# Rotation left to the scores' contraction, the last down part in token halves, and two buffers placed at multiples of 2048 bytes

## The chip, the cores and the metric

The kernel runs on one core of one Trainium2 chip. The metric is the time of the device in microseconds for one launch; the time before is the median of three runs. TensorE is called PE below, VectorE DVE, ScalarE ACT, GpSimd POOL and SyncE SP, as the profile calls them.

## The reference, cut to what matters

One layer of a trunk, on a sequence of 512 tokens with 1024 channels, all in float32:

```python
x = x + 0.5 * swiglu(rms_norm(x, ffn1_norm), ffn1_w1, ffn1_w3, ffn1_w2)     # hidden width 2816
h = rms_norm(x, mix_norm)
proj = h @ w_in
c_q, c_kv, k_pe, q_s, k_s, v_s = jnp.split(proj, IN_SPLIT_POINTS, axis=-1)
y_mla = mla_attention(c_q, c_kv, k_pe, cos, sin, ...) @ w_o_mla             # 8 heads, 64 nope + 32 rope
y_swa = swa_attention(q_s, k_s, v_s, rel_bias, sinks) @ w_o_swa             # 16 heads, banded
g_mla, g_swa = jnp.split(sigmoid(h @ w_gate), 2, axis=-1)
x = x + (g_mla * y_mla + g_swa * y_swa) @ w_out
x = x + 0.5 * swiglu(rms_norm(x, ffn2_norm), ffn2_w1, ffn2_w3, ffn2_w2)
out = rms_norm(x, final_norm)
```

In the latent attention (MLA) a head's query is 64 plain numbers and 32 that are rotated: `q_pe = x1*cos - x2*sin, x2*cos + x1*sin`. The score of a query and a key is the sum over the 96. The rotated key is shared by all heads.

## The kernel before

The state x lies transposed, channels on the 128 partitions (8 tiles of 128x512, tokens along the free dimension). Each float32 product is made of three matmuls in the type float32r with a high and a low part of both operands (`three`, L1098: high by high L1101, weights' high by low L1102, weights' low by high L1103), each 128x128 weights by 128x512 moving, added in a PSUM bank. A "product" is one output tile: 8 such triples in the up projections, 8 or 6 in the down ones. A weight tile ("unit") is loaded by SP into one of four buffers `staged` (a load waits for `lo_done` of the unit four before), its high part is made by ACT (L508), its low part by DVE (L740), 1024 columns each, in two buffers `w_hi`, `w_lo`.

The program is in order: feed-forward 1 (PARTS of 8, 8 and 6 hidden tiles: for each part the up products, then 8 down products that are added to x), the mixing part, feed-forward 2 likewise, and the last norm. The hidden tiles are made by DVE (L802), rounded by ACT to `h_hi` (L531), and POOL makes `h_lo` (L395); `h_ready` counts POOL's.

In the mixing part the order is written out by hand: 48 steps of attention (16 banded, then 32 of MLA) run on PE, and behind each step PE does "fillers" of a plan (`fillers`, L63), products that have nothing to do with the step: latent projections, `kpe` (the shared rotary key), `uk`, `uv`, `uq` (the queries of head t, three triples), gates. In step n PE does the scores of step n + 2 (L1220 for MLA), the transposes of the probabilities of step n (L1252), the values, and the fillers. DVE in the same step normalises the probabilities of step n + 1 (L923, L924 for MLA), adds the mask and takes the maximum of step n + 2 (L901 to L903), splits a weight unit, and does its share of the fillers. For `uq` of head t, PSUM holds 64 plain rows, 32 rows of the rotary part and the same 32 swapped by halves. ACT copies the 64 rows (L668), DVE multiplies the 32 by the cosines (L984) and the swapped 32 by the signed sines into `rot` (L990), and POOL adds `rot` (L462, `q_ready`):

```python
nc.vector.tensor_tensor(qm[lo, t, :], b[lo, :], rope_sb[lo, :], ALU.mult)
...
dve.wait_ge(q_nope, t + 1)
nc.vector.tensor_tensor(rot[lo, :], b[hi, :], rope_sb[hi, :], ALU.mult).then_inc(grp_read, 1)
```

DVE's L990 of head t waits for ACT's copy of head t and for POOL's add of head t - 1. The scores read 96 rows of `qm` and `km`.

At the end, each of the 8 down products of the last part is added to x by DVE (L815); ACT squares it (L513) and scales it by the gain (L546); POOL adds the squares (L377). After the last one: PE sums over channels (L1154, L1393, one column each), DVE makes the variance (L754, L1088), POOL the power -0.5 (L387), DVE a Newton step (L770 to L773) and a diagonal (L775), PE spreads it over the partitions (L1162), ACT copies it (L732), DVE and POOL multiply the 8 tiles (L1094, L488), and SP sends them in six transfers (L360).

`h_hi` and `h_lo` start at an odd multiple of 64 bytes (a small tile `lead` is put in front and their alignment is 64), `lat_hi` and `lat_lo` at a multiple of 256; the other operands of the matmuls (`xg_hi`, `summed`, `om`, `w_hi`) start at multiples of LINE = 2048 bytes.

## Time and profile before

| | |
|---|---|
| median of 3 runs | 1160.23 us (1160.18 to 1160.59) |
| the profiled execution: its time | 1159.75 us |
| its span, first to last instruction | 1158.0 us |
| PE busy | 1127.8 us (97%) |
| DVE, ACT, POOL busy | 585.6, 400.9, 182.0 us |
| granted clock of PE, mean | 0.994 |
| chain that ended last | PE 91%, DVE 4%, ACT 2%, issue 1% |

The time of the profiled execution is 1.75 us more than its span, and 0.48 us under the median. A busy PE is not PE at its peak: records of matmuls overlap (each of 128x512 is shown as 0.39 us long while they start 0.23 us apart), so the pace of PE is read from starts. Weight loads (PEld) have records of their own.

### The profile page before, as it was taken

The numbers are of one execution on the slowest core, as the hardware profiler recorded it, in microseconds if no ns is written. First come the engines' busy times: TensorE is split into PE (matmuls) and PEld (weight loads), VectorE is DVE, ScalarE is ACT, GpSimd is POOL, SyncE is SP. The second block draws the span as 40 slices with busy tenths as digits, with TensorE's granted clock in tenths as the row PEclk, the third lists the DMA queues.
The fourth block names the chain that finished last, engine by engine and source line by source line (L and its number), as shares of the span: only waits on it lengthen the run. The fifth ranks groups of instructions, "written<-read, shape, count | busy, mean of one in ns | idle before, by whom it ended". The sixth has DMA issues, their size and how long they took to land.

```text
span 1158.0 us, 14717 instructions
## 1 busy us (share of the span) xinstructions
PE 1127.8 (97%) x5110; PEld 908.9 (78%) x5110; DVE 585.6 (51%) x870; ACT 400.9 (35%) x693; POOL 182.0 (16%) x134
## 2 busy tenths in 40 slices
PE   6999999999999999998999999999999999999995
PEld 4888888888888887765777788888888888888883
DVE  6644344433446436788555564545453344434444
ACT  5322123322325225584444433332231232222242
POOL 4111011100113103323000002231110011101133
PEclk9999999999999999999999999999999999999997
DMA  6234332333224321111222132222332322332221
GB/s 217 91 105 101 112 101 99 91 97 103 91 69 131 99 102 46 56 41 51 73 73 74 55 103 98 91 98 88 105 91 91 106 93 91 98 102 91 78 67 73
DMA packets 32301, 105.43 MB, mean 91 GB/s; under 512 B 3888, under 2 KB 5328, under 8 KB 32256
## 3 DMA queue, kind: packets, MB, share of 16 engines
q1 hardware_dynamic: 31824, 104.02, 27.9%
q0 software_dynamic: 192, 0.78, 0.6%
q8 instruction: 25, 0.41, 0.2%
q14 instruction: 20, 0.16, 0.0%
q10 hardware_dynamic: 240, 0.05, 0.0%
HBM read 101.96 MB, written 2.88 MB: 91 GB/s over the span
## 4 chain that ended last, share of the span: by engine, by line
PE 91%; DVE 4%; ACT 2%; issue 1%; POOL 0%; DMA 0%; DVEq 0%; SPq 0%; POOLq 0%; ACTq 0%
PE bank L1101 29%; PE bank L1103 28%; PE bank L1102 28%; PE bank L1220 1%; PE bank L1252 1%; PE bank L1277 1%; DVE xg_lo L747 1%; PE bank L1210 1%; ACT probs L607 1%; PE bank L1162 0%; DMA x<-in_x_t 0%; DVE w_lo L740 0%; DVE x L1094 0%; PE bank L1262 0%; DVE rot L990 0%
## 5 line engine op out<-in xcount | busy, mean ns | idle before, releaser
L1101 PE MATMUL bank<-xg_hi,w_hi 128*128 128x512 f32 (+1 forms) x1024 | 406.6, 397 | 10.1 <-DVE xg_lo L747 8.6
L508 ACT ACTIVATE w_hi<-staged 128x1024 fp32r<-128x1024 f32 x192 | 203.5, 1060 | 583.5 <-PE bank L1103 583.5
L1103 PE MATMUL bank<-xg_hi,w_lo 128*128 128x512 f32 (+1 forms) x1024 | 399.7, 390 | 0.0
L1102 PE MATMUL bank<-xg_lo,w_hi 128*128 128x512 f32 (+1 forms) x1024 | 399.7, 390 | 0.0
L740 DVE TENSOR_TENSOR w_lo<-staged,w_hi 128x1024 fp32r<-128x1024 f32 x192 | 236.7, 1233 | 101.2 <-ACT w_hi L508 100.9
L1101 PEld LDWEIGHTS bank<-xg_hi,w_hi 128*128 128x128 f32 (+1 forms) x1024 | 192.1, 188 | 58.9 <-issue 14.0
L1103 PEld LDWEIGHTS bank<-xg_hi,w_lo 128*128 128x128 f32 (+1 forms) x1024 | 192.3, 188 | 41.4
L1102 PEld LDWEIGHTS bank<-xg_lo,w_hi 128*128 128x128 f32 (+1 forms) x1024 | 192.4, 188 | 39.4 <-issue 0.7
L395 POOL TENSOR_TENSOR h_lo<-hid,h_hi 128x512 f32 x44 | 71.2, 1619 | 568.0 <-ACT h_hi L531 539.2
L1101 PE MATMUL bank<-h_hi,w_hi 128*128 128x512 f32 x352 | 138.8, 394 | 0.2
L1103 PE MATMUL bank<-h_hi,w_lo 128*128 128x512 f32 x352 | 137.7, 391 | 0.0
L1102 PE MATMUL bank<-h_lo,w_hi 128*128 128x512 f32 x352 | 137.2, 390 | 0.0
L815 DVE SCALAR_TENSOR_TENSOR x<-bank,x 128x512 f32 (+1 forms) x56 | 38.7, 691 | 152.9 <-PE bank L1103 152.9
L787 DVE TENSOR_TENSOR a_rms<-bank,rms 128x512 f32<-128x512 f32 x44 | 30.4, 691 | 118.9 <-PE bank L1103 118.8
L1103 PEld LDWEIGHTS bank<-h_hi,w_lo 128*128 128x128 f32 x352 | 66.1, 188 | 15.3
L1101 PEld LDWEIGHTS bank<-h_hi,w_hi 128*128 128x128 f32 x352 | 66.2, 188 | 14.7 <-POOL h_lo L395 1.1
L1102 PEld LDWEIGHTS bank<-h_lo,w_hi 128*128 128x128 f32 x352 | 66.1, 188 | 14.3
L377 POOL TENSOR_TENSOR acc<-acc,sq 128x512 f32<-128x512 f32 x36 | 56.9, 1580 | 95.3 <-ACT sq L513 84.4
L802 DVE TENSOR_TENSOR hid<-bank,silu 128x512 f32<-128x512 f32 x44 | 30.4, 692 | 79.1 <-PE bank L1103 78.7
L478 POOL TENSOR_TENSOR summed<-probs,summed 128x512 f32 x8 | 10.3, 1292 | 182.5 <-ACT summed L726 182.5
L620 ACT ACTIVATE probs_t<-bank 128x512 f32<-128x512 f32 (+3 forms) x48 | 23.4, 488 | 33.5 <-PE bank L1252 25.5
L792 DVE SCALAR_TENSOR_TENSOR silu<-silu,a_rms 128x512 f32<-128x512 f32 x44 | 31.6, 718 | 2.8 <-ACT silu L560 2.8
(131 smaller groups left out, 892.7 us busy)
## 6 DMA issues: line engine op xcount, KB each, us to landing
staged<-in_ffn_w SPq DMA_DIRECT2D x119, 512.0 KB, 3.3
staged<-in_w_gate SPq DMA_DIRECT2D x16, 512.0 KB, 3.3
staged<-in_w_in SPq DMA_DIRECT2D x15, 512.0 KB, 3.3
staged<-in_ffn_w SPq DMA_DIRECT2D x16, 384.0 KB, 3.1
staged<-in_w_ob SPq DMA_DIRECT2D x8, 512.0 KB, 3.3
staged<-in_w_out SPq DMA_DIRECT2D x8, 512.0 KB, 3.2
x<-in_x_t SPq DMA_DIRECT2D x8, 256.0 KB, 5.9
staged<-in_w_oa SPq DMA_DIRECT2D x4, 512.0 KB, 3.2
```

The costliest lines, as they stand in the source:

```text
L377: pool.tensor_tensor(acc[:, n % 2, :], acc[:, n % 2, :], sq[:, s % 2, :], ALU.add)\
L395: pool.tensor_tensor(h_lo[:, 2 * i + j, :], hid[:, (fb + j) % 2, :], h_hi[:, 2 * i + j, :].bitcast(f32), ALU.subtract)\
L508: nc.scalar.activation(w_hi[:, u % SPLIT, :], staged[:, u % STAGED, :], ACT.Copy).then_inc(hi_done, 1)
L620: nc.scalar.activation(probs_t[:, n % 2, 0:cols], bank[T_BANK + n % 2][:, 0:cols], ACT.Copy)\
L740: nc.vector.tensor_tensor(w_lo[:, u % SPLIT, :], staged[:, u % STAGED, :], w_hi[:, u % SPLIT, :].bitcast(f32), ALU.subtract).then_inc(lo_d ...
L787: nc.vector.tensor_tensor(a_rms[:, j, :], bank[g % 4][:, :], rms[:, :], ALU.mult).then_inc(grp_read, 1)
L792: nc.vector.scalar_tensor_tensor(out=silu[:, j, :], in0=silu[:, j, :], scalar=1.0, in1=a_rms[:, j, :], op0=ALU.add, op1=ALU.mult).then_inc ...
L802: nc.vector.tensor_tensor(hid[:, j, :], bank[g % 4][:, :], silu[:, j, :], ALU.mult).then_inc(grp_read, 1)
L815: nc.vector.scalar_tensor_tensor(out=x[:, k, :], in0=bank[(g + j) % 4][:, :], scalar=factor, in1=x[:, k, :], op0=ALU.mult, op1=ALU.add).th ...
L1101: nc.tensor.matmul(o, wh, hi, start=start, stop=False)
L1102: nc.tensor.matmul(o, wh, lo, start=False, stop=False)
L1103: return nc.tensor.matmul(o, wl, hi, start=False, stop=stop)
```

## The change

There are three edits.

**Rotation.** The weights of `uq` are as before, but `rope_sb` now holds ones in rows 0 to 63, cosines in 64 to 95 and signed sines in 96 to 127, and one multiplication of all 128 rows makes `qm`. The two rotary parts are not added; `km` holds the rotated key twice (rows 64 to 95 and 96 to 127), and the scores contract over 128 rows, which adds them. ACT's copy, DVE's second multiplication and POOL's addition are gone, with `q_nope` and `q_ready`. For the key, the `kpe` weights are 128 columns wide instead of 64, and DVE copies 64 rows for each head after a first copy of 32.

**Last down part.** Feed-forward 2's last down part is done for tokens 0 to 255 and then for 256 to 511 (`half`), each of its 16 products 18 matmuls of 256 columns. The split weights of all 8 units are kept in `end_hi` and `end_lo` (768 columns). The last norm of the first half is done between products of the second.

**Buffers.** `h_hi`, `h_lo`, `lat_hi` and `lat_lo` are aligned to LINE.

```diff
-            sb("lead", [P, 16], f32, ffn)
-            h_hi = sb("h_hi", [P, max(PARTS), S], f32r, ffn, align=64)
-            h_lo = sb("h_lo", [P, max(PARTS), S], f32r, ffn, align=64)
+            h_hi = sb("h_hi", [P, max(PARTS), S], f32r, ffn, align=LINE)
+            h_lo = sb("h_lo", [P, max(PARTS), S], f32r, ffn, align=LINE)
...
-            sb("lat_lead", [P, 64], f32, r)
-            lat_hi = sb("lat_hi", [P, 5, S], f32r, r, align=256)
-            lat_lo = sb("lat_lo", [P, 5, S], f32r, r, align=256)
+            lat_hi = sb("lat_hi", [P, 5, S], f32r, r, align=LINE)
+            lat_lo = sb("lat_lo", [P, 5, S], f32r, r, align=LINE)
...
-                elif kind == "uq":
-                    alone(q_ready, t + 1)
-                    pool.wait_ge(grp_read, MIX_G + G_UQ + t + 1)
-                    pool.tensor_tensor(qm[rope_rows, t, :], qm[rope_rows, t, :], rot[rope_rows, :], ALU.add)\
-                        .then_inc(q_ready, 1)
...
-                elif kind == "uq":
-                    act.wait_ge(grp_ready, g + G_UQ + t + 1)
-                    nc.scalar.activation(qm[0:NOPE, t, :], filler_bank(G_UQ + t)[0:NOPE, :], ACT.Copy)\
-                        .then_inc(q_nope, 1)
...
-                    nc.vector.tensor_tensor(qm[lo, t, :], b[lo, :], rope_sb[lo, :], ALU.mult)
-                    if t >= 1:
-                        dve.wait_ge(q_ready, t)
-                    else:
-                        dve.wait_ge(kpe_ready, 1)
-                    dve.wait_ge(q_nope, t + 1)
-                    nc.vector.tensor_tensor(rot[lo, :], b[hi, :], rope_sb[hi, :], ALU.mult).then_inc(grp_read, 1)
+                    nc.vector.tensor_tensor(qm[:, t, :], filler_bank(G_UQ + t)[:, :], rope_sb[:, :], ALU.mult)\
+                        .then_inc(grp_read, 1)
...
-                        pe.wait_ge(q_ready, h + 1)
-                        pe.wait_ge(kpe_ready, MH)
-                    rows = slice(0, NOPE + ROPE)
-                    nc.tensor.matmul(b[:, 0:query_keys(i)], qm[rows, h, norm_rows(i)], km[rows, h, 0:query_keys(i)],
+                        pe.wait_ge(grp_read, g + G_UQ + h + 1)
+                        pe.wait_ge(kpe_ready, MH + 1)
+                    nc.tensor.matmul(b[:, 0:query_keys(i)], qm[:, h, norm_rows(i)], km[:, h, 0:query_keys(i)],
                                      start=True, stop=True).then_inc(s_ready, 1)
...
+            def end_product(half, k):
+                n = KD * half + k
+                pe.wait_ge(lo_done, LAST_U + k + 1)
+                if n < 4:
+                    pe.wait_ge(grp_read, LAST_G - 3 + n)
+                else:
+                    pe.wait_ge(end_read, n - 3)
+                o = bank[(LAST_G + n) % 4][:, 0:HALF]
+                for f in range(LAST_F):
+                    if n == 0:
+                        pe.wait_ge(h_ready, 2 * sum(PARTS) - LAST_F + f + 1)
+                    w_cols = slice(f * P, (f + 1) * P)
+                    hi, lo = h_hi[:, f, half_cols(half)], h_lo[:, f, half_cols(half)]
+                    nc.tensor.matmul(o, end_hi[:, k, w_cols], hi, start=f == 0, stop=False)
+                    nc.tensor.matmul(o, end_hi[:, k, w_cols], lo, start=False, stop=False)
+                    last = nc.tensor.matmul(o, end_lo[:, k, w_cols], hi, start=False, stop=f == LAST_F - 1)
+                last.then_inc(end_ready, 1)
...
+            for half in range(HALVES):
+                for k in range(KD):
+                    end_product(half, k)
+                    if half == 1 and k == 1:
+                        sum_end(0)
+                    if half == 1 and k == 3:
+                        spread_end(0)
+            sum_end(1)
+            spread_end(1)
```

ACT in the end, for each half and tile, and DVE and POOL likewise:

```python
            for half in range(HALVES):
                for k in range(KD):
                    if half == 0 and k + AHEAD < KD:
                        end_split(k + AHEAD)
                    n = KD * half + k
                    act.wait_ge(end_read, n + 1)
                    if k >= 2:
                        act.wait_ge(end_acc, (KD - 1) * half + k - 1)
...
                    nc.scalar.activation(sq_end[:, k % 2, :], x[:, k, half_cols(half)], ACT.Square).then_inc(end_sq, 1)
                    nc.scalar.activation(x[:, k, half_cols(half)], x[:, k, half_cols(half)], ACT.Copy,
                                         scale=gain[:, 3 * KD + k, :]).then_inc(out_scaled, 1)
                    if half == 1 and k == 4:
                        read_rms_end(0)
            read_rms_end(1)
```

**Where instructions move.** DVE in one step of MLA with a `uq` filler, before (L923, L924 normalise, L901 to L903 mask and maximum, L984 and L990 the filler):

```order
L923 RECIPROCAL rden<-den 128x1
L924 TENSOR_SCALAR probs<-probs,rden 128x256
L901 TENSOR_TENSOR bank<-bank,mask_sb 128x128
L902 TENSOR_REDUCE smax<-bank 128x1
L903 TENSOR_SCALAR nmax<-smax 128x1
L740 TENSOR_TENSOR w_lo<-staged,w_hi 128x1024
L984 TENSOR_TENSOR qm<-bank,rope_sb 32x512
L990 TENSOR_TENSOR rot<-bank,rope_sb 32x512
```

The same step after:

```order
L989 RECIPROCAL rden<-den 128x1
L990 TENSOR_SCALAR probs<-probs,rden 128x256
L967 TENSOR_TENSOR bank<-bank,mask_sb 128x128
L968 TENSOR_REDUCE smax<-bank 128x1
L969 TENSOR_SCALAR nmax<-smax 128x1
L806 TENSOR_TENSOR w_lo<-staged,w_hi 128x1024
L1052 TENSOR_TENSOR qm<-bank,rope_sb 128x512
```

One of the filler's two instructions is gone, and the other has 128 rows instead of 32; POOL's `L462 TENSOR_TENSOR qm<-qm,rot 32x512` (8 of them) and ACT's 8 copies are gone too.

PE at the end of the program, before, from the last triple on:

```order
L1101 MATMUL bank<-h_hi,w_hi 128x512
L1102 MATMUL bank<-h_lo,w_hi 128x512
L1103 MATMUL bank<-h_hi,w_lo 128x512
L258 REGISTER_ALU
L258 COMPARE_AND_BRANCH
L1154 MATMUL bank<-one,acc 128x1 x4
L1393 MATMUL bank<-one,sq 128x1 x4
L1162 MATMUL bank<-diag,one 128x512
```

And after:

```order
L1510 MATMUL bank<-h_hi,end_hi 128x256
L1511 MATMUL bank<-h_lo,end_hi 128x256
L1512 MATMUL bank<-h_hi,end_lo 128x256
L1518 MATMUL bank<-one,acc_end 128x1 x2
L1523 MATMUL bank<-one,sq_end 128x1 x2
L1530 MATMUL bank<-diag,one 128x256
```

The last three rows stand in this place for the second half alone; the same for the first half stands between products of the second: L1518 and L1523 behind its second product, L1530 behind its fourth.

DVE at the end, before, from the last read of a product on:

```order
L815 SCALAR_TENSOR_TENSOR x<-bank,x 128x512 x2
L754 TENSOR_SCALAR var<-bank 128x4
L1088 SCALAR_TENSOR_TENSOR var<-bank,var 128x4
L770 TENSOR_TENSOR corr<-rstd 128x4
L771 SCALAR_TENSOR_TENSOR corr<-corr,var 128x4
L773 SCALAR_TENSOR_TENSOR rstd<-corr,rstd 128x4
L775 TENSOR_TENSOR diag<-idn,rstd 128x512
L1094 TENSOR_TENSOR x<-x,rms 128x512 x6
```

And after, from the third product of the second half on:

```order
L1193 SCALAR_TENSOR_TENSOR x<-bank,x 128x256 x4
L1184 TENSOR_TENSOR x<-x,rms 128x256 x6
L1193 SCALAR_TENSOR_TENSOR x<-bank,x 128x256 x2
L1164 TENSOR_SCALAR var<-bank 128x2
L1168 SCALAR_TENSOR_TENSOR var<-bank,var 128x2
L1171 TENSOR_TENSOR corr<-rstd 128x2
L1172 SCALAR_TENSOR_TENSOR corr<-corr,var 128x2
L1174 SCALAR_TENSOR_TENSOR rstd<-corr,rstd 128x2
L1176 TENSOR_TENSOR diag<-idn,rstd 128x256
L1184 TENSOR_TENSOR x<-x,rms 128x256 x6
```

The six multiplications of the first half (L1184) now stand ahead of the reads of the last two products.

## Rows read from the trace of the kernel before

**Rows 1.** Timeline of PE, an up part: start us, us, engine, line, operation.
```profile
925.43 0.39 PE L1101 MATMUL bank<-xg_hi,w_hi 128*128 128x512 f32 x1
...
939.71 0.39 PE L1101 MATMUL bank<-xg_hi,w_hi 128*128 128x512 f32 x1
```
**Rows 2.** Timeline of PE, a down part.
```profile
1005.08 0.39 PE L1101 MATMUL bank<-h_hi,w_hi 128*128 128x512 f32 x1
...
1019.50 0.39 PE L1101 MATMUL bank<-h_hi,w_hi 128*128 128x512 f32 x1
```
**Rows 3.** Busy time in a stretch: width, PE, PEld, DVE, ACT, POOL, PE's clock.
```profile
505.00:548.00 43.00, 36.94 (x177) 25.87 (x176) 36.01 (x75) 24.23 (x72) 14.27 (x12) 1.00 0.13 44
```
**Rows 4.** Groups of 505 to 548 us: busy us, mean ns, idle before.
```profile
L462 POOL TENSOR_TENSOR qm<-qm,rot 32x512 f32<-32x512 f32 x8 | 10.1, 1264 | 23.2 <-DVE rot L990 23.2
...
L990 DVE TENSOR_TENSOR rot<-bank,rope_sb 32x512 f32<-32x512 f32 x8 | 5.6, 696 | 2.3 <-ACT qm L668 1.7 <-POOL qm L462 0.5
L984 DVE TENSOR_TENSOR qm<-bank,rope_sb 32x512 f32<-32x512 f32 x8 | 5.5, 689 | 2.7 <-ACT vm L665 2.2 <-PE bank L1103 0.2
...
L902 DVE TENSOR_REDUCE smax<-bank 128x1 f32<-128x256 f32 x2 | 0.8, 424 | 0.1
```
**Rows 5.** Timeline of one `uq` step, and of a later L924 with POOL idle.
```profile
535.00 0.81 PE L1220 MATMUL bank<-km,qm 96*128 96x384 f32 x2
...
535.57 1.25 POOL L462 TENSOR_TENSOR qm<-qm,rot 32x512 f32<-32x512 f32 x1 [3.08 <-DVE rot L990]
535.66 1.32 DVE L924 TENSOR_SCALAR probs<-probs,rden 128x256 f32<-128x256 f32 x1
...
537.03 0.44 PE L1252 MATMUL bank<-idn,probs 128*128 128x128 f32 x2 [1.23 <-DVE probs L924]
...
549.12 0.42 DVE L924 TENSOR_SCALAR probs<-probs,rden 128x384 f32<-128x384 f32 x1
```
**Rows 6.** Timeline: the start of the last down part.
```profile
1106.80 0.40 PE L1101 MATMUL bank<-h_hi,w_hi 128*128 128x512 f32 x1
...
1108.83 1.65 POOL L395 TENSOR_TENSOR h_lo<-hid,h_hi 128x512 f32 x1 [9.24 <-ACT h_hi L531]
...
1110.53 0.50 PE L1101 MATMUL bank<-h_hi,w_hi 128*128 128x512 f32 x1
```
**Rows 7.** Page, groups: ACT's split of a unit.
```profile
L508 ACT ACTIVATE w_hi<-staged 128x1024 fp32r<-128x1024 f32 x192 | 203.5, 1060 | 583.5 <-PE bank L1103 583.5
```
**Rows 8.** Chain of work: sums and spread behind the first feed-forward (start, us, what).
```profile
388.14 0.79 PE bank L1154 x8
...
394.54 0.86 PE bank L1162 x2
```
**Rows 9.** Timeline: the end of the program.
```profile
1139.95 0.39 PE L1103 MATMUL bank<-h_hi,w_lo 128*128 128x512 f32 x1
...
1140.37 0.69 DVE L815 SCALAR_TENSOR_TENSOR x<-bank,x 128x512 f32<-128x512 f32 x1 [3.43 <-PE bank L1103]
1141.16 0.63 ACT L513 ACTIVATE sq<-x 128x512 f32<-128x512 f32 x1 [2.87 <-DVE x L815]
...
1141.84 0.97 PEld L1393 LDWEIGHTS bank<-one,sq 128*128 128x128 f32 x8 [0.80 <-ACT sq L513]
...
1143.24 1.02 POOL L387 TENSOR_TENSOR rstd<-var,minus_half 128x4 f32<-128x4 f32 x1 [4.14 <-DVE var L1088]
...
1144.88 0.69 DVE L775 TENSOR_TENSOR diag<-idn,rstd 128x512 f32<-128x512 f32 x1
...
1145.63 2.08 PE L1162 MATMUL bank<-diag,one 128*128 128x512 f32 x2 [2.74 <-DVE diag L775]
1147.74 0.60 ACT L732 ACTIVATE rms<-bank 128x512 f32<-128x512 f32 x1 [5.34 <-PE bank L1162]
1148.37 5.84 DVE L1094 TENSOR_TENSOR x<-x,rms 128x512 f32<-128x512 f32 x6 [2.80 <-ACT rms L732]
```
**Rows 10.** Busy time in a stretch, as in rows 3: the spread of the last norm.
```profile
1145.60:1148.00 2.40, 2.08 (x2) 0.50 (x2) 0.00 (x0) 0.26 (x1) 0.00 (x0) 0.50 0.01 3
```

More of the change, by code:

```diff
@@ L247, in trunk_layer @@
         POOL_OUT = (6, 7)
+        DVE_OUT = tuple(k for k in range(KD) if k not in POOL_OUT)
+        END_SUM, END_RMS = (7, 5), (6, 4)
+        END_COLS = TT // HALVES
         M_SCALE = float(NOPE + ROPE) ** -0.5
@@ L401, in ffn_program @@
                         bring()
-                clear_acc(n)
-                if n == NORM_OUT:
-                    for t in range(KD - 1):
-                        add_square(n, t)
-                else:
+                if n is not None:
+                    clear_acc(n)
                     loop(pool, 2, lambda i: [add_square(n, t, i) for t in range(4)], first=1)
@@ L1290, in next_bank, with half_product @@
                 return filler_bank(r)
-            def half_product(uu, r, half, width=P):
+            def half_product(uu, r, half):
                 if half == 0:
@@ L1297, in half_product @@
                 for k in range(4 * half, 4 * half + 4):
-                    last = three(filler_bank(r)[0:width, :], slice(k * width, (k + 1) * width), uu, *from_x(k),
-                                 k == 0, k == KD - 1)
+                    last = three(filler_bank(r)[:, :], slice(k * P, (k + 1) * P), uu, *from_x(k), k == 0, k == KD - 1)
                 if half == 1:
@@ L1389, in _ @@
             ffn_program(FFN2_U, FFN2_G, sum(PARTS), 2, NORM_X2)
-            sum_squares(NORM_OUT)
-            pe.wait_ge(sq_done, sq_base[NORM_OUT + 1])
-            for t in range(TT):
-                last = nc.tensor.matmul(bank[RMS_BANK][:, t:t + 1], sq[:, (sq_base[NORM_OUT + 1] - 1) % 2, norm_rows(t)],
-                                        one[:, 0:1], start=True, stop=True)
-            last.then_inc(ss_ready, 1)
-            spread_rms(NORM_OUT)
+            def end_product(half, k):
+                n = KD * half + k
+                pe.wait_ge(lo_done, LAST_U + k + 1)
[13 more added lines that the diff above has]
+                last.then_inc(end_ready, 1)
@@ new lines, in sum_end @@
+            def sum_end(half):
+                pe.wait_ge(end_acc, (KD - 1) * (half + 1))
+                for t in range(END_COLS):
+                    last = nc.tensor.matmul(bank[END_SUM[half]][:, t:t + 1], acc_end[:, half, norm_rows(t)], one[:, 0:1],
+                                            start=True, stop=True)
+                last.then_inc(end_summed, 1)
+                pe.wait_ge(end_sq, KD * (half + 1))
+                for t in range(END_COLS):
+                    last = nc.tensor.matmul(bank[END_RMS[half]][:, t:t + 1], sq_end[:, (KD - 1) % 2, norm_rows(t)],
+                                            one[:, 0:1], start=True, stop=True)
+                last.then_inc(end_summed, 1)
@@ new lines, in spread_end @@
+            def spread_end(half):
+                pe.wait_ge(end_diag, half + 1)
+                cols = diag[:, half * END_COLS:(half + 1) * END_COLS, :].rearrange("p a b -> p (a b)")
+                nc.tensor.matmul(bank[END_RMS[half]][:, 0:HALF], one[:, :], cols, start=True, stop=True)\
+                    .then_inc(end_spread, 1)
+            for half in range(HALVES):
+                for k in range(KD):
+                    end_product(half, k)
+                    if half == 1 and k == 1:
+                        sum_end(0)
+                    if half == 1 and k == 3:
+                        spread_end(0)
```

220 lines of the change are left out of this document (157 added, 63 removed).

## The prediction

> **What bounds the kernel now.** I read the page first. PE is busy for 97% of the span and makes 91% of the chain that ended last, and its clock is full nearly throughout. So the kernel is a stream of matmuls, and only three things can move its time: the pace of the stream, the places where it stops, and what lies behind its last matmul.
>
> The pace is read from starts in the timeline of PE. In an up part, the first and the last row of [rows 1] are 63 matmuls apart (21 triples): 14.28 us, 226.7 ns each. In a down part [rows 2] the same 63 take 14.42 us, 228.9 ns each. The weights come from the same buffers in both; the moving operand is `xg`, at a multiple of 2048 bytes, in the first and `h`, at a multiple of 64, in the second. Neither stretch has a wait in it.
>
> The stops come from the busy time by stretch. From 505 to 548 us, where the `uq` fillers are, PE is busy for 36.94 of 43 us, and DVE for 36.01 [rows 3]. The timeline of one step [rows 5] shows why: PE has done its scores (two passes from 535.00, 0.65 us by the 0.81 shown less the overlapping drain), and the transposes start at 537.03, since DVE's L924 ends only at 536.98. That L924 took 1.32 us for 256 columns; with POOL idle the same instruction took 0.42 for 384. It overlaps POOL's L462 (535.57 to 536.82), so the two hold each other up. DVE is therefore late by its own two filler instructions (0.69 and 0.70 us) and by about 1.0 us that POOL costs it [rows 4, 5].
>
> The end is in [rows 9]: the last matmul of the down part starts at 1139.95 and is over at 1140.34. The span ends at 1158.0, so 17.7 us lie behind it, a chain through all engines on tiles of 512 tokens.
>
> **The change, term by term.** The sum is made against the profiled execution (1159.75 us; span 1158.0), which lies 0.48 us under the median of the runs.
>
> *Buffers.* The two feed-forwards have 1056 matmuls that read `h`; 912 of them keep 512 columns. If the 2.2 ns come from where `h` starts, they save 912 x 2.2 = 2.0 us. Bounds: 0 (the cause is another) and 2.3 (`lat` gains likewise). I take **-2.0**, because both stretches are without waits and differ in the moving operand alone.
>
> *Rotation.* Of a `uq` step DVE loses L990 (0.70) and its wait for ACT's copy, and L924 loses POOL's company (about 1.0). The instruction that stays is as long with 128 rows as with 32, by the nearest rows: L984 on 32 rows takes 689 ns [rows 4] and L775 on 128 rows 0.69 us [rows 9]. Over 8 heads this is some 13 us of DVE's 36, so DVE has 23 us of work in a stretch in which PE has 37. PE can get back at most its idle 6.1 us (43 - 36.94) [rows 3]; none at least, if another wait takes its place. A step's latency (maximum, exponential, normalisation) is spread over two steps, so I take nearly all: **-5.5**. The wider `kpe` weights and one more copy of the key fall where PE was not idle; I cost them at nothing, and at 0.7 us (one DVE instruction [rows 4]) if DVE's slack there is used up.
>
> *Late hidden tile.* The first product of the last down part needs the sixth hidden tile behind 15 matmuls. Before, that is at 1106.80 + 15 x 0.229 = 1110.24, and POOL's `h_lo` ends at 1110.48, so PE went on at 1110.53 after a stop of 0.29 [rows 6]. Now 15 matmuls of half the length are over at 1108.5, and the tile is still made for all 512 tokens. The stop becomes 2.0: **+1.7** (1.4 if ACT, which no longer waits for a free `w_hi`, rounds the tile earlier; 2.3 if POOL is held up by DVE's four splits in a row).
>
> *Pace at 256 columns.* 288 matmuls take the place of 144 at 228.9 ns (33.0 us). The stream alone would allow half of 226.7, 113.3 ns. Each also needs its own 128x128 weights. The loads behind one another at the end [rows 9] are 8 in 0.97 us, the last 0.19 long: (0.97 - 0.19)/7 = 111 ns apart. So the floor is 111. The other bound: at 512 columns each start is 13.4 ns more than 512 columns at 2.4 GHz (213.3); if that is a price of each matmul rather than of each column, 256 columns take 120. Between 111 and 120 I take 116: 33.4 us, **+0.4** (-1.0 to +1.6).
>
> Here a rule speaks against the change. The rows show loads hidden under the stream: at 226.7 ns apart there is no room for 213 of columns and 111 of weights [rows 1, 9]. The Trainium skill (TensorE: Matmul & The Clock Gate, Part 3, "The mechanism") says that loads overlap running matmuls only where the row groups differ, and all here use all rows; by that each matmul would pay for both. The trace at 512 columns disagrees with it; at 256 columns no row shows it, and it stands as a rival below.
>
> *Inserted work.* Between products of the second half PE now does the sums of the first (8 one-column passes, like L1154 x8: 0.79) and its spread at half width (half of L1162's 0.86 at full clock) [rows 8]: 1.2, and 0.1 for each change of kind, **+1.4** (1.2 to 2.0). DVE's and ACT's work on the first half lies beside PE's products. What is queued behind DVE's first norm (its waits for PE's sums and POOL's power, about 2.5 us) is the read of the third product, which PE needs free only two products later.
>
> *The end.* From the end of the last matmul, the new chain: read of 256 columns 0.45 (a DVE instruction on 256 columns takes 0.42 [rows 4]); 0.35 late, since DVE has just done six multiplications of the first half and ACT's squares lag; square 0.5; sums 0.7; to POOL's start 0.4; power 1.0; Newton step 0.6; diagonal 0.45; spread 1.2, half of 2.08 and a little, if PE's clock has dropped to 1.2 GHz by then as it had before [rows 10]; copy 0.4; multiplications half of 5.84, 2.9; from there to the end of the span 3.8 before (1158.0 - 1154.2), and with transfers of 384 KB in place of 512 I take 3.6 [rows 9]. The sum is 12.55, for 17.7: 5.1 less. I take **-5.0** (-3.5 if the first half's work makes the last reads 1.5 us late; -6.0 if the spread is at full clock and the transfers gain more).
>
> *Weights of the last part.* A product now takes 18 x 0.116 = 2.1 us instead of 4.1, and in the first half ACT must split a unit (768 columns: 0.85 by L508's 1.06 for 1024 [rows 7]), square and scale: 1.75. DVE needs 0.95 and 0.42. Both fit under 2.1; four units are split ahead. Nothing is charged.
>
> Sum: -2.0 - 5.5 + 1.7 + 0.4 + 1.4 - 5.0 = **-9.0 us**, 1150.75 for a profiled execution, and 1160.23 - 9.0 = **1151.2** for the median.
>
> **The rivals.**
>
> *A (the mixing part keeps its stops).* PE's wait for the probabilities could turn into one for the exponentials, ACT being in the same loop. For it: ACT's splits of 1.06 us stand in the same steps. Against: ACT was busy for only 24.2 of the 43 us. Then the rotation gives 1.5 instead of 5.5: 1155.2.
>
> *B (no gain from the buffers).* 2.2 ns could come from how a down part is built (6 or 8 triples a product). Against: the extra is in every triple, not at a product's start. Then 1153.2.
>
> *C (the last part is bound by its weights or by ACT).* At 1.75 of 2.1 us ACT has 0.35 to spare, and loads of 384 KB now have to come every 2.1 us. If four products are late by 1 us each: 1155.2.
>
> *D (slower: loads stop being hidden).* A load's record is 188 ns long, and if the next matmul waits for its end, the spacing is about 188: 288 x (188 - 116) = +20.7, 1172. If stream and load come one after another (113 + 111 = 224), it is 288 x 108 = +31, 1182; this is what the rule above would give. Against the first: loads start 111 ns apart while 0.19 long. D decides from a spacing of 116 + 9000/288 = 147 ns on; under that the change stays faster.
>
> *E (nothing comes of it).* Rotation and end both give half: 2.7 + 2.5 + 2.0 - 3.5 = 3.7 less, 1156.5; with dearer inserted work it comes within 0.2% (2.3 us, about what a measurement of this kernel can tell from no change).
>
> **How the numbers follow.** Forecast 0.56, A 0.12, B 0.10, C 0.06, D 0.07 (stream and load one after another 0.02 of it), E 0.09. The bounds of the terms give the forecast 1148 to 1154 (buffers 0.3, rotation 0.6, late tile 0.6, pace 1.3, end 1.5, taken together and not all on one side). Holding A, B, C and most of E and the low bounds a little further, the range is 1146.5 to 1157.0. Faster is all but D and a half of E: 0.88; same (the other half) 0.05; slower 0.07.
>
> **What would show it.** Right: matmuls of a down part 226.7 ns apart; PE busy for all of the `uq` stretch and L990 (the old L924) at 0.4 us; POOL without the additions; a stop of about 2 us before the sixth triple of the last part; 256-column matmuls 111 to 120 ns apart; 12 to 13 us behind the last of them. Wrong: `h` still at 228.9; transposes waiting for DVE or ACT in the `uq` steps; a spacing of 147 ns or more; ACT or a load as what ends PE's waits in the last part.

## The result and the profile after

| | before | after |
|---|---|---|
| median of the runs | 1160.41 us (1160.18 to 1160.61, 4 runs) | 1148.55 us (1147.53 to 1149.57, 4 runs) |
| profiled execution: time, span | 1159.75, 1158.0 us | 1149.52, 1147.7 us |
| PE busy | 1127.8 us (97%) | 1125.6 us (98%) |
| POOL, DVE busy | 182.0, 585.6 us | 170.5, 574.7 us |

The ratio is 0.9899, with an interval of 0.9887 to 0.9911: the changed kernel is 1.0% faster, 11.9 us by the medians. 1151.2 was forecast, in a range of 1146.5 to 1157.0. One of the 15 runs of the kernel before beside experiments 7 and 8 took 1267.34 us, at a granted clock of 0.848, and is left out of their ratios.

The stretch of [rows 3], the same 43 us of the profile after (columns as there):

```profile
505.00:548.00 43.00, 42.98 (x219) 32.03 (x219) 30.47 (x80) 24.43 (x73) 4.05 (x4) 1.00 0.15 52
```

PE has no stop left in it, and POOL's additions are gone. The normalisation of the probabilities on DVE (L924 before, L990 now), by form, in the same stretch:

```profile
L990 DVE TENSOR_SCALAR probs<-probs,rden 128x384 f32<-128x384 f32 x2 | 0.8, 420 | 0.1
```

It takes 0.42 us for 384 columns; 256 of them took 1.32 beside POOL's addition [rows 5].

A down part, timeline of PE, against [rows 2]: 63 matmuls in 14.28 us, 226.7 ns each.

```profile
1002.00 0.39 PE L1208 MATMUL bank<-h_hi,w_hi 128*128 128x512 f32 x1
...
1016.28 0.39 PE L1208 MATMUL bank<-h_hi,w_hi 128*128 128x512 f32 x1
```

The last down part, timeline: its first matmul, POOL's making of the sixth hidden tile, the matmul that waited for it, 36 matmuls of the stream (120.0 ns each), and the work inserted between products of the second half.

```profile
1097.88 0.28 PE L1510 MATMUL bank<-h_hi,end_hi 128*128 128x256 f32 x1
...
1099.63 1.27 POOL L415 TENSOR_TENSOR h_lo<-hid,h_hi 128x512 f32 x1 [8.91 <-ACT h_hi L568]
...
1100.96 0.39 PE L1510 MATMUL bank<-h_hi,end_hi 128*128 128x256 f32 x1 [1.13 <-POOL h_lo L415]
...
1115.10 0.28 PE L1510 MATMUL bank<-h_hi,end_hi 128*128 128x256 f32 x1
...
1119.42 0.28 PE L1510 MATMUL bank<-h_hi,end_hi 128*128 128x256 f32 x1
...
1120.86 0.50 PE L1518 MATMUL bank<-one,acc_end 128*128 128x1 f32 x4
1121.22 0.58 PE L1523 MATMUL bank<-one,sq_end 128*128 128x1 f32 x4
1121.67 0.36 PE L1510 MATMUL bank<-h_hi,end_hi 128*128 128x256 f32 x1
...
1126.06 0.60 PE L1530 MATMUL bank<-diag,one 128*128 128x256 f32 x2
```

The end, timeline, against [rows 9]:

```profile
1135.01 0.28 PE L1512 MATMUL bank<-h_hi,end_lo 128*128 128x256 f32 x1
...
1135.32 0.42 DVE L1193 SCALAR_TENSOR_TENSOR x<-bank,x 128x256 f32<-128x256 f32 x1 [0.52 <-PE bank L1512]
...
1135.78 0.42 ACT L787 ACTIVATE sq_end<-x 128x256 f32<-128x256 f32 x1
...
1137.51 0.71 POOL L509 TENSOR_TENSOR rstd<-var,minus_half 128x2 f32<-128x2 f32 x1 [1.45 <-DVE var L1168]
...
1139.32 1.22 PE L1530 MATMUL bank<-diag,one 128*128 128x256 f32 x2 [2.15 <-DVE diag L1176]
...
1140.99 3.16 DVE L1184 TENSOR_TENSOR x<-x,rms 128x256 f32<-128x256 f32 x6 [1.73 <-ACT rms L772]
```

From the end of the last matmul (1135.28) to that of the span 12.4 us are left, where there were 17.7.

### The profile page after: what moved, and what is told of

Same layout as the page of the kernel before. It is cut to its first block, busy times and chain, and to the rows that moved or that the text cites. A ratio compares the mean times of both kernels' runs of the same rounds, so it can differ in the third digit from the quotient of the medians.

```text
span 1147.7 us, 14995 instructions
## 1 busy us (share of the span) xinstructions
PE 1125.6 (98%) x5256; PEld 918.0 (80%) x5256; DVE 574.7 (50%) x883; ACT 398.6 (35%) x702; POOL 170.5 (15%) x136
## 4 chain that ended last, share of the span: by engine, by line
PE 95%; DVE 3%; ACT 1%; issue 0%; DMA 0%; POOL 0%; DVEq 0%; SPq 0%; POOLq 0%; ACTq 0%
PE bank L1208 29%; PE bank L1210 28%; PE bank L1209 28%; PE bank L1328 2%; PE bank L1360 1%; PE bank L1385 1%; PE bank L1319 1%; PE bank L1510 1%; DVE xg_lo L813 1%; PE bank L1512 1%; PE bank L1511 1%; PE bank L1370 1%; DVE x L1184 0%; DMA staged<-in_ffn_w 0%; PE bank L1269 0%
## 5 line engine op out<-in xcount | busy, mean ns | idle before, releaser
L1208 PE MATMUL bank<-xg_hi,w_hi 128*128 128x512 f32 x1024 | 406.8, 397 | 10.1 <-DVE xg_lo L813 8.6
L1210 PE MATMUL bank<-xg_hi,w_lo 128*128 128x512 f32 x1024 | 399.7, 390 | 0.0
L1209 PE MATMUL bank<-xg_lo,w_hi 128*128 128x512 f32 x1024 | 399.6, 390 | 0.0
L1208 PEld LDWEIGHTS bank<-xg_hi,w_hi 128*128 128x128 f32 x1024 | 192.6, 188 | 59.1 <-issue 14.2
L1210 PEld LDWEIGHTS bank<-xg_hi,w_lo 128*128 128x128 f32 x1024 | 192.6, 188 | 40.9
L1209 PEld LDWEIGHTS bank<-xg_lo,w_hi 128*128 128x128 f32 x1024 | 192.8, 188 | 39.1 <-issue 0.7
L415 POOL TENSOR_TENSOR h_lo<-hid,h_hi 128x512 f32 x44 | 70.8, 1610 | 565.4 <-ACT h_hi L568 537.0
L1208 PE MATMUL bank<-h_hi,w_hi 128*128 128x512 f32 x304 | 118.4, 389 | 0.2 <-POOL h_lo L415 0.2
L1209 PE MATMUL bank<-h_lo,w_hi 128*128 128x512 f32 x304 | 118.3, 389 | 0.0
L1210 PE MATMUL bank<-h_hi,w_lo 128*128 128x512 f32 x304 | 118.3, 389 | 0.0
L881 DVE SCALAR_TENSOR_TENSOR x<-bank,x 128x512 f32 x48 | 33.2, 691 | 134.7 <-PE bank L1210 134.7
L1208 PEld LDWEIGHTS bank<-h_hi,w_hi 128*128 128x128 f32 x304 | 57.1, 188 | 12.4 <-POOL h_lo L415 0.6
L1209 PEld LDWEIGHTS bank<-h_lo,w_hi 128*128 128x128 f32 x304 | 57.1, 188 | 11.9
```

What stands on the lines that cost most here:

```text
L415: pool.tensor_tensor(h_lo[:, 2 * i + j, :], hid[:, (fb + j) % 2, :], h_hi[:, 2 * i + j, :].bitcast(f32), ALU.subtract)\
L881: nc.vector.scalar_tensor_tensor(out=x[:, k, :], in0=bank[(g + j) % 4][:, :], scalar=factor, in1=x[:, k, :], op0=ALU.mult, op1=ALU.add).th ...
L1208: nc.tensor.matmul(o, wh, hi, start=start, stop=False)
L1209: nc.tensor.matmul(o, wh, lo, start=False, stop=False)
L1210: return nc.tensor.matmul(o, wl, hi, start=False, stop=stop)
```

## The experiments

Medians of kernels on different chips differ by more than some of the effects. So two lengths are read from each profiled execution as well: **A**, from the start of the fifth `xg_lo` on DVE (13.90 us in the profile before) to the end of the span, and **B**, the middle part, from the last addition to x of feed-forward 1 (377.36) to the first of the attention's output (741.90). Two executions of the changed kernel agree in both within 0.1 us.

| kernel | A, us | B, us |
|---|---|---|
| before | 1144.1 | 364.5 |
| buffers alone | 1142.6 | 365.7 (clock) |
| last part alone | 1143.4 | 365.7 (clock) |
| rotation alone | 1137.0 | 357.6 |
| rotation, POOL's addition back | 1138.1 | 358.7 |
| rotation, DVE's multiplication back | 1138.7 | 359.3 |
| rotation, both back | 1141.1 | 361.3 |
| rotation, both and ACT's copy back | 1144.2 | 364.8 (clock) |
| changed; again | 1133.5; 1133.5 | 357.6; 357.6 |
| changed, two products together | 1132.3 | 357.6 |

"(clock)": PE's granted clock fell to half for a while at 523 us. It costs 1.15 us of B (365.7 - 364.5, in two kernels that leave that part's order alone), and is told of below. A "stop" is an idle time of PE of 0.1 us or more in the stretch of [rows 3]; the one near 505 us, for DVE's `lat`, is in all kernels and is not counted.

**1. Buffers alone.**

```diff
-            h_hi = sb("h_hi", [P, max(PARTS), S], f32r, ffn, align=64)
+            h_hi = sb("h_hi", [P, max(PARTS), S], f32r, ffn, align=LINE)
...
-            lat_hi = sb("lat_hi", [P, 5, S], f32r, r, align=256)
+            lat_hi = sb("lat_hi", [P, 5, S], f32r, r, align=LINE)
```

> The kernel before with the third edit alone: h and lat at multiples of 2048 bytes. Theory (where the moving operand starts sets the pace): every matmul on h is 226.7 ns behind the last instead of 228.9, 1056 of them, so 2.3 us less, about 1158.0. Rival (the pace in a down part comes from how a down product is built, and the change got its gain elsewhere): 228.9 stays and the time is 1160.3.

Measured: 1157.68 us (10 runs) beside 1161.12 (19 runs), ratio 0.9975 (0.9965 to 0.9984). The same 63 matmuls of a down part, timeline of PE:

```profile
1003.18 0.39 PE L1099 MATMUL bank<-h_hi,w_hi 128*128 128x512 f32 x1
...
1017.46 0.39 PE L1099 MATMUL bank<-h_hi,w_hi 128*128 128x512 f32 x1
```

226.7 ns each: where `h` starts is the cause of the 2.2 ns. The products on `lat` did not change: nine matmuls from 514.2 us on are 228.8 ns apart before and nine from 513.1 us on 228.6 here. A is 1.5 less, and 2.6 with the clock's 1.15 taken out.

**2. Rotation alone.**

> The kernel before with the first edit alone. Theory (the stops of the uq steps are all DVE being late, by its second filler instruction and by POOL's addition): PE is busy for 43 of the 43 us from 505 to 548 and the time falls by 6.9 us, what the trace of the changed kernel shows between the end of the first feed-forward and the last values of the attention: about 1153.4. Rival (part of it was from the buffer lat or came with the other edits): 1154.5 to 1157.

Measured: 1153.43 us (4 runs) beside 1161.12, ratio 0.9942 (0.9926 to 0.9959); B is 6.9 us less. Busy time of the stretch with the same 177 records of PE as [rows 3]:

```profile
505.40:541.50 36.10, 35.58 (x177) 26.28 (x177) 26.74 (x71) 21.24 (x66) 4.17 (x4) 1.00 0.19 64
```

43.00 us have become 36.10, and that is all of B's gain. PE's idle time went from 6.06 to 0.52 us, and its busy time fell by 1.36 too, for the same matmuls.

The kernel before has seven stops in its stretch that are gone here. Three, in steps of MLA (537.03, 542.12 and 546.83, together 3.25 us), end with DVE's L924, as the prediction read from one step. The other four, 2.62 us together, end with POOL. They are in the last two banded steps, in which POOL makes the normalisation (L442), in its program order behind the addition of `uq` (L462). This is the second of them, in the kernel before:

```profile
521.16 1.26 POOL L462 TENSOR_TENSOR qm<-qm,rot 32x512 f32<-32x512 f32 x1 [3.34 <-DVE rot L990]
521.24 0.18 DVE L918 RECIPROCAL rden<-den 128x4 f32<-128x4 f32 x1
...
522.49 1.04 POOL L442 TENSOR_TENSOR probs<-probs,rden 128x512 f32<-128x512 f32 x1
522.52 0.46 PE L1220 MATMUL bank<-km,qm 96*128 96x128 f32 x2 [1.14 <-issue]
...
523.59 0.66 PE L1252 MATMUL bank<-idn,probs 128*128 128x128 f32 x4 [0.61 <-POOL probs L442]
```

L442 has its operand at 521.42 and starts at 522.49, behind L462. The stop of 1.14 us ends with L462 too: these are a head's first scores, in front of which the program waits for `q_ready`, and they start 0.1 us after L462's end. In the step before, the two stops are 0.26 and 0.61 us.

**3. Last part alone.**

> The kernel before with the second edit alone, h where it was. Theory: the last part costs 4.0 us more up to its last matmul (288 starts 120 ns apart in place of 144 at 228.9: +1.6; late hidden tile +1.0; sums and spread of the first half +1.3) and 5.3 us less lie behind it: -1.3, about 1159.0, perhaps less if the half steps are dearer with h at 64 bytes. Rival (the gain behind the last matmul is bigger in unprofiled runs, which for the changed kernel came out at 1147.5 or at 1149.5): two groups of times 2 us apart, 1157 and 1159.

Measured: 1159.24 us (10 runs) beside 1161.12, ratio 0.9989 (0.9979 to 0.9998). A is 0.7 less, 1.8 with the clock's 1.15 taken out. That is 0.4 more than the edit gives in the changed kernel (its terms below sum to -1.4). Here `h` still starts off by 64 bytes, and 36 matmuls of the last part (timeline of PE) are 117.8 ns apart in place of 120.0; experiment 9 takes this up. The ten runs lie in two groups, 1157.98 to 1158.40 (four, with a mean granted clock of 0.996) and 1159.00 to 1159.85 (six, with 0.995, the profiled one among them), so that the fall of the clock at 523 us (1.15 us) is nearly enough to tell them apart; the rival's groups, 2 us apart by what lies behind the last matmul, are not shown.

```profile
1115.23 0.28 PE L1527 MATMUL bank<-h_hi,end_hi 128*128 128x256 f32 x1
...
1119.47 0.28 PE L1527 MATMUL bank<-h_hi,end_hi 128*128 128x256 f32 x1
```

**4. The pace by itself.** Behind the spread of the last norm:

```diff
+            def run(count, cols, off, w=P, w_off=0):
+                for m in range(count):
...
+                    nc.tensor.matmul(bank[m // 12 % 4][0:w, 0:cols], wt[:, 0, w_off + tile * P:w_off + tile * P + w],
+                                     mv[:, tile * S + off:tile * S + off + cols], start=True, stop=True)
```

> The kernel before with 17 rows of matmuls added behind its last one, whose results nobody reads: 512, 384, 256, 192, 128 and 64 moving columns, moving operands that start 4, 16, 64, 256 columns off a multiple of 512 columns, weights of 64 columns, weights that start off a multiple of 128 columns. Theory (a matmul costs its columns at 2.4 GHz and a fixed 13.4 ns, and never less than the load of its weights, 111 ns): 226.7, 173.4, 120.0, then 111 for 192 (93.4), 128 and 64. Rival (the extra is 1/16 of the columns): 226.7, 170, 113.3, 111. With a start off the multiple by 16 or 64 columns: 228 to 230 by the theory of the buffers, 226.7 by its rival.

Measured, mean spacing of starts in a series (weights of 128 columns, start at a multiple of 2048 bytes, where nothing else is said):

| series | ns |
|---|---|
| 512, 384, 256 columns | 226.7, 173.3, 120.0 |
| 192, 128 columns | 111.7, 111.7 |
| 512 columns, moving operand off by 16, 64, 256, 1024 bytes | 231.6, 228.9, 226.7, 226.7 |
| 512 columns, weights off by 64, 256 bytes | 233.4, 226.7 |
| 512, 256 columns, weights of 64 columns | 230.0, 113.3 |

The series at 256 bytes starts with ten matmuls some 232 ns apart, behind the slower series before it, and is at 226.7 from then on.

From 512 to 256 columns the spacing falls by 106.7 ns, which is 256 columns at 2.4 GHz; so each matmul costs its columns and a fixed 13.3 ns, and the other way of sharing the 13.4 ns out (a price of each column), which the prediction gave weight, is refuted. At 192 and 128 columns the floor of 111.7 rules. What the fixed price is paid for is not shown: with weights of half as many columns it goes at 256 moving columns (113.3 ns), and at 512 it does not (230.0 ns, more than with full weights). Rival D is refuted: a matmul of 256 columns is 120.0 ns after the last with a load of 128x128 of its own, not 188 and not 113 + 111. With it falls, for these matmuls that use all rows, the rule of the Trainium skill (TensorE: Matmul & The Clock Gate, Part 3, "The mechanism") that was weighed in the prediction.

**5. POOL's addition back.** The rotation alone, and on POOL behind each `uq`:

```diff
+                elif kind == "uq":
+                    alone(spare_done, t + 1)
+                    pool.wait_ge(grp_read, MIX_G + G_UQ + t + 1)
+                    pool.tensor_tensor(rot[rope_rows, :], rot[rope_rows, :], rot[rope_rows, :], ALU.add)\
+                        .then_inc(spare_done, 1)
```

> The rotation alone (as in the run before), and POOL has an addition of 32x512 again behind every one of the 8 uq fillers, in a tile that nobody reads; it is work that is added, nothing is left out. Theory: POOL's addition and DVE's normalisation of the probabilities hold each other up, and this is the larger part of what the rotation gave. Then the normalisation in the uq steps goes from 0.37 back to about 1.3 us, the addition takes 1.25 instead of some 0.4 to 1.0, and the kernel is 1.5 to 4 us slower than the rotation alone. Rival: what counted was DVE's second multiplication and its waits, and PE's slack of about 1.2 us in these steps takes the 0.9 us in; then it is under 0.8 us slower, though the normalisation is at 1.3 us again.

Measured: 1154.32 us (4 runs) beside 1160.07 (7 runs), ratio 0.9951 (0.9934 to 0.9967); B is 1.1 us over the rotation alone. The stretch of [rows 3] and the group of the normalisation in it:

```profile
505.00:548.00 43.00, 41.73 (x201) 30.42 (x201) 33.98 (x79) 24.10 (x71) 12.42 (x12) 1.00 0.19 62
```
```profile
L920 DVE TENSOR_SCALAR probs<-probs,rden 128x128 f32<-128x128 f32 (+3 forms) x7 | 6.7, 960 | 0.2
```

0.96 us in the mean in place of 0.37: the hold-up is back, and PE does not feel it, for no step of MLA has a stop. The 1.1 us come from POOL's other work. There are two stops, 0.17 and 0.57 us, in the last two banded steps, where POOL's normalisation again stands behind its addition (the second of them):

```profile
519.80 1.03 POOL L462 TENSOR_TENSOR rot<-rot 32x512 f32<-32x512 f32 x1 [2.17 <-DVE qm L982]
...
520.91 1.04 POOL L442 TENSOR_TENSOR probs<-probs,rden 128x512 f32<-128x512 f32 x1
...
522.01 0.66 PE L1244 MATMUL bank<-idn,probs 128*128 128x128 f32 x4 [0.57 <-POOL probs L442]
```

The theory that the hold-up of DVE is the larger part of the gain falls.

**6. DVE's second multiplication back**, without POOL's addition:

```diff
+                    nc.vector.tensor_tensor(rot[NOPE:NOPE + ROPE, :], filler_bank(G_UQ + t)[NOPE + ROPE:P, :],
+                                            rope_sb[NOPE + ROPE:P, :], ALU.mult).then_inc(grp_read, 1)
```

> The rotation alone, and DVE has its second multiplication of 32x512 again behind every uq filler, in a tile that nobody reads, without ACT's copy and without POOL's addition; it is work that is added, nothing is left out. Theory (the lock of POOL and DVE is the larger part): 8 x 0.70 = 5.6 us more of DVE's work meet a slack of about 1.2 us in every step, and the kernel is 0 to 1.5 us slower than the rotation alone. Rival (DVE's work as such is the larger part): 1.5 to 4 us slower, with PE waiting for the normalised probabilities again. Third way: neither this nor POOL's addition alone costs over 0.8 us, and the stops came only from both together.

Measured: 1154.63 us (4 runs), ratio 0.9954 (0.9937 to 0.997); B 1.6 us over the rotation alone.

```profile
505.00:548.00 43.00, 41.84 (x202) 30.68 (x201) 35.35 (x84) 24.51 (x73) 4.12 (x4) 1.00 0.16 55
```

It is not the larger part either: 1.1 and 1.6, of 6.9. Again no step of MLA has a stop. The two stops, 0.11 and 1.03 us, are in the last two banded steps, where POOL's normalisation waits for DVE's L908, which comes later.

**7. Both back** (the edits of 5 and 6, and DVE's next one waits for POOL's last):

> The rotation alone, with both additions of the two runs before it: DVE's second multiplication and, behind it, POOL's addition, each in a tile that nobody reads; DVE's next one waits for POOL's last one as it did before the change. It is work that is added, nothing is left out. From the start of the attention steps on, POOL's addition alone cost 1.1 us and DVE's multiplication alone 1.6; the whole that the rotation took away is worth 6.9. Theory: the two costs lie behind one slack in every step (about 1.2 us), so each alone is mostly hidden and both together are not: 0.7 + 0.95 a step less the slack. Then the middle part is 4.5 to 7 us longer than in the rotation alone, and the normalisation is at 1.3 us in every uq step. Rival: the costs simply add to 2.7 us, and the other 4 us of the rotation come from something else: ACT's copy of 64 rows and DVE's wait for it.

Measured: 1156.99 us (6 runs) beside 1160.85 (15 runs), ratio 0.9967 (0.9955 to 0.998); B 3.7 us over the rotation alone, between the 2.7 of a plain sum and the 4.5 that the theory wanted at least. The stops are 0.87 and 1.30 us in the banded steps and 0.95 in one step of MLA, for DVE's normalisation; with either alone that step had none.

```profile
505.00:548.00 43.00, 39.49 (x189) 28.67 (x190) 37.48 (x81) 21.99 (x68) 12.42 (x12) 1.00 0.16 56
```

**8. Both and ACT's copy of 64 rows**, with DVE's wait for it:

```diff
+                elif kind == "uq":
+                    act.wait_ge(grp_ready, g + G_UQ + t + 1)
+                    nc.scalar.activation(qm[0:NOPE, t, :], filler_bank(G_UQ + t)[0:NOPE, :], ACT.Copy)\
+                        .then_inc(copied, 1)
...
+                    dve.wait_ge(copied, t + 1)
```

> As the run before it, and ACT copies the 64 plain rows again (DVE multiplies only the other 64), with DVE's second multiplication waiting for the copy. What is left of the rotation edit is the contraction over 128 rows and the wider key; nothing is left out. Theory: ACT's copy of 0.58 us ends 0.2 us after DVE's first multiplication started beside it and adds 0 to 1.5 us to the run with both; the middle part comes within 1 us of that of the kernel before (6.9 us over the rotation alone). Rival: ACT's copy is where the missing 4 us were, and this run is 3 us or more over the one with both.

Measured: 1158.99 us (10 runs) beside 1160.85, ratio 0.9987 (0.9978 to 0.9997). B is 364.8, 363.6 with the clock's 1.15 taken out: 6.0 over the rotation alone, 0.9 short of the kernel before. ACT's copy with its wait is worth 2.3 us on top of both, more than the theory allowed (1.5) and less than the rival wanted (3). So no part carries the gain alone: taken back one after another they cost 1.1 (POOL), 2.6 (DVE on top), 2.3 (ACT's copy on top) and 0.9 (the rest). That rest goes with POOL's additions: on one tile they take 1.03 us here, on two 1.26 before [rows 4], and the normalisation is held up less, 1.09 for 1.32; that this is all of it was not tried. The stops say where it lies. In the banded steps they are as long here (0.87 and 1.76 us) as before (0.87 and 1.75), though PE's own wait for POOL's addition, `q_ready`, is not back; so that wait costs nothing. In the three steps of MLA they are 0.28, 1.14 and 0.44 us, where the kernel with the buffers alone, which had the same fall of the clock, has 0.81, 1.36 and 0.66: 0.97 less.

**9. Starts and widths.** As 4, with other series:

> The kernel before, with 492 further matmuls of 128x128 weights whose results nobody reads, between the spread of the last norm and its use, in series of 36 with one width and one start of the moving operand: it is work that is added, nothing is left out. Open is why the last part runs at 117.8 ns a matmul of 256 columns where h starts at an odd multiple of 64 bytes (the run with the last part alone) and at 120.0 where it starts at a multiple of 2048. Theory: the start counts at 256 columns too, but the other way round: 118 ns for a start off by 64 bytes and 120 for one off by 0, with 226.7 and 228.9 at 512 columns again. Rival: the start has nothing to do with it and the 2 ns come from what runs beside the last part, or from the changing weights; then all series of 256 columns are at 120.0.

Measured: the theory's numbers. Timeline of PE, pairs of rows 24 matmuls apart, 256 columns with a start off by 0 and by 64 bytes, and 512 with a start off by 0, 64 and 128 bytes:

```profile
1164.31 0.28 PE L1405 MATMUL bank<-xg_hi,w_hi 128*128 128x256 f32 x1
...
1167.19 0.28 PE L1405 MATMUL bank<-xg_hi,w_hi 128*128 128x256 f32 x1
...
1168.62 0.28 PE L1405 MATMUL bank<-xg_hi,w_hi 128*128 128x256 f32 x1
...
1171.45 0.28 PE L1405 MATMUL bank<-xg_hi,w_hi 128*128 128x256 f32 x1
...
1203.17 0.39 PE L1405 MATMUL bank<-xg_hi,w_hi 128*128 128x512 f32 x1
...
1208.61 0.39 PE L1405 MATMUL bank<-xg_hi,w_hi 128*128 128x512 f32 x1
...
1211.36 0.39 PE L1405 MATMUL bank<-xg_hi,w_hi 128*128 128x512 f32 x1
...
1216.85 0.39 PE L1405 MATMUL bank<-xg_hi,w_hi 128*128 128x512 f32 x1
...
1219.62 0.39 PE L1405 MATMUL bank<-xg_hi,w_hi 128*128 128x512 f32 x1
...
1225.20 0.40 PE L1405 MATMUL bank<-xg_hi,w_hi 128*128 128x512 f32 x1
```

That is 120.0, 117.8, 226.7, 228.8 and 232.5 ns. At 384 columns both starts give 173.3. So the edit of the buffers costs the last part 288 x 2.2 = 0.6 us of what it gives elsewhere.

**10. The late hidden tile out of the way**, in the changed kernel:

```diff
+            end_product(0, 0, range(LAST_F - 1))
+            end_product(0, 1, range(LAST_F - 1))
+            end_product(0, 0, (LAST_F - 1,))
+            end_product(0, 1, (LAST_F - 1,))
```

> The changed kernel, with the sixth hidden tile's triples of the first two products of the last down part done together: five tiles of product 0, five of product 1, then the sixth of each. Nothing is left out. The stop before the sixth tile is 1.29 us in the changed kernel (15 matmuls are over at 1099.7, the tile is there at 1100.9). With 30 matmuls ahead of it, PE gets there at 1097.9 + 30 x 0.120 = 1101.5, 0.6 us after the tile, so the stop should go to nothing: 1.3 us less than the changed kernel run beside it. Rival: the first reads by DVE and squares by ACT come 0.4 us later, and that or a weight unit that is split late gives the time back further on; then the two kernels are the same within 0.5 us, with a new wait for DVE or ACT in the first half of the last part.

Measured: 1146.84 us (4 runs: three at 1146.8, one at 1148.23) beside 1149.17 for the changed kernel, ratio to before 0.989 (0.9873 to 0.9906). A is 1.2 us less, as the theory had it, and the idle time before the group of the last part's first matmuls, 1.1 us in the changed kernel, is gone:

```profile
L1510 PE MATMUL bank<-h_hi,end_hi 128*128 128x256 f32 x95 | 27.3, 287 | 0.0
```

The other 1.1 us of the 2.3 lie in the first 14 us of the program and are told next.

**11. The changed kernel again.**

> The changed kernel again, unaltered, beside the others. Its four runs lay in two groups, 1147.5 and 1149.5 us. Theory: the two groups are its own and not the chip's, so it shows them here too, 2 us apart, and the profile of one of the lower group would show the place. Rival: they were the chip's, and all runs here lie within 0.5 us of each other.

Measured: 1149.17 us (1149.14 to 1149.65, 4 runs), ratio 0.9907 (0.9891 to 0.9924). All four lie within 0.5 us and none at 1147.5: the theory that the two groups are the kernel's own is not borne out, and no trace shows the lower group. The timeline of the first weight splits still shows one way in which executions come apart. POOL and DVE here:

```profile
11.39 1.48 POOL L395 TENSOR_TENSOR acc<-acc,sq 128x512 f32<-128x512 f32 x1 [0.23 <-ACT sq L550]
11.64 2.31 DVE L806 TENSOR_TENSOR w_lo<-staged,w_hi 128x1024 fp32r<-128x1024 f32 x1
```

And in the profile of experiment 10:

```profile
11.59 1.21 DVE L806 TENSOR_TENSOR w_lo<-staged,w_hi 128x1024 fp32r<-128x1024 f32 x1
...
12.09 1.86 POOL L395 TENSOR_TENSOR acc<-acc,sq 128x512 f32<-128x512 f32 x1 [0.97 <-ACT sq L550]
```

Where POOL is first, DVE's split ends 1.08 us after POOL's operation (13.95 and 12.87); where DVE is first, POOL's ends 1.15 after the split. The start of the program, where tiles of x arrive by DMA, decides which is first, and everything behind is 1.1 us earlier or later.

## Why the prediction came out right, step by step

The profiled executions differ by 10.2 us (A by 10.6), where the sum said 9.0. The medians differ by 11.9: most of before's runs in these comparisons lie between 1160 and 1161.5 us and the profile of before at 1159.75, so the profile that the sum was made against was one of the quicker ones. That of the changed kernel, 1149.52, was one of its slower ones; the median of 1148.55 lies between the two groups. That the sum of the terms is off by 1.6 us and the median by 2.7 is in part this choice of executions.

- **Buffers, -2.0.** Right in mechanism and size: 1.2 us less up to the end of feed-forward 1, and 1.0 in feed-forward 2 up to the last part, -2.2. Rival B is refuted by experiment 1.
- **Rotation, -5.5: the term mis-sized most, -6.9.** The step that failed is the bound, "PE can get back at most its idle 6.1 us". It got back 5.5 of these and 1.4 that the rows show as busy. A record of 0.39 us outlasts the 0.227 after which the next one starts; at a stop these 0.16 us are no longer covered by a next record. Seven stops went, 7 x 0.16 = 1.1. The second matmul behind a stop was late by another 0.06 to 0.08 us when the starts of both kernels are compared one by one, together 0.4: 1.5, about the 1.4 measured. That the stops go and no other wait takes their place came true, and rival A is refuted by the stretch without a stop. The account of what made them was right in part. The step that was read, at 535 us, stands for three steps of MLA and 3.25 us; the other 2.62 us were for POOL's own instructions in two banded steps (experiment 2). The price of POOL's company was charged in all 8 steps, though L924 stands in the stretch only five times: DVE lost 9.3 us of busy time (36.01 to 26.74), not 13. Experiments 5 to 8 show three parts: POOL's addition, DVE's multiplication and ACT's copy. Neither of the first two gives a stop in a step of MLA when it is alone; together they give one, and with the copy three.
- **Late hidden tile, +1.7.** Measured 1.3 of stop in place of 0.3, +1.0: POOL's L415 began 1.75 us behind the part's first matmul instead of 2.03, and took 1.27 us in place of 1.65 [rows 6], since DVE's split of a unit beside it (1108.09 to 1109.31 before) is of 768 columns now and over at 1099.64, as POOL starts.
- **Pace at 256 columns, +0.4.** Measured 120.0 ns, the upper bound and not 116: 288 x 120.0 - 144 x 228.9 = +1.6. Experiment 4 shows that the 13.4 ns are a price of each matmul.
- **Inserted work, +1.4.** 0.89 for the sums (1121.67 - 1120.86, and the pace) and 0.43 for the spread: 1.3.
- **The end, -5.0.** 12.4 us for 17.7, -5.3. The power took 0.71 in place of the 1.0 charged, and the additions and squares were 0.1 to 0.2 earlier. The spread took 1.22 at a clock of 0.51, as forecast.
- **Weights of the last part.** No wait of PE in it is for weights or ACT; rival C did not come.

The sum of the measured terms is -2.2 - 6.9 + 1.0 + 1.6 + 1.3 - 5.3 = -10.5, against 10.6 less in A. The forecast's 9.0 came nearer than its parts, because the pace and the rotation erred on opposite sides.

What stays open: why four runs of the changed kernel fell at 1147.5 and 1149.5. The order of POOL and DVE at the start would explain 1.1 us of such a difference. The mean granted clock was 0.997 in the two lower runs and 0.996 in the two upper ones, so the clock may have a part in it. No trace shows either.

## What to carry to other kernels

An engine's idle time in the profile is not the upper bound of what the removal of its stops gives: each stop also costs the part of a record that the next one would have covered. When several small helpers stand in front of one slack, take them out together; each alone is mostly hidden (1.1 and 1.6 us of 6.9 here). Read every stop of a stretch before pricing it by one of them: here two engines ended PE's waits, and POOL's addition, when it was back alone, cost PE time only as what stood in front of POOL's own next instruction. Splitting a stream of matmuls in halves costs a fixed price for each additional matmul (13.3 ns, 1.6 us here with 144 more matmuls), and a product that has to wait for its last operand is best interleaved with the next one.

## What the runs showed of the hardware

- **The start of an operand changes the pace of PE**, by width: a moving operand of 512 columns takes 226.7 ns at a multiple of 2048 bytes and when off by 256, 512 or 1024, 232.5 when off by 128, 228.9 by 64 and 231.6 by 16. One of 256 columns takes 120.0 where it is not off, and less, 117.8, where it is off by 64. Weights off by 64 bytes cost 6.7 ns.
- **POOL and DVE take turns.** The one that starts second ends only after the first, in experiment 11 by the 1.1 us that it needs alone. The Trainium skill (SBUF — State Buffer, "Who interferes with whom") says that whichever starts first holds a port pair they share for its whole instruction, for a DVE operation with two SBUF inputs or in a two-port mode; the traces agree, with 1.21 and 2.31 us for one and the same split.
- **PE's clock at 523 us.** The kernel before, and those that keep its stops, have six microseconds with PE busy for 4.2 of them. In some executions the granted clock then falls, as in this one (last part alone):

```profile
520.00:523.00 3.00, 1.82 (x8) 1.06 (x7) 2.47 (x7) 1.66 (x6) 1.79 (x2) 1.00 0.51 175
523.00:526.00 3.00, 2.43 (x9) 1.35 (x10) 2.55 (x5) 1.52 (x3) 1.77 (x2) 0.60 0.00 0
```

In the profile before it stayed at 1.00 with the same stops. The 0.60 is time spent partly at 1.2 GHz, and B is 1.15 us longer. Four of the five profiles with all seven stops show it (experiments 1, 3, 4 and 9), so does that of experiment 8 with five, and no profile of a kernel with three of them or fewer shows a fall there, so the change seems to take this cost, too, from those executions of before that have it. A fall where PE has time to spare costs nothing: in the profile of experiment 11 the clock is at half from 14.0 us on for a while, and A is 1133.5, as without it.
